# x transposed on the host for the first unit, its rows loaded later, and other banks for the third and fourth units

## What is computed

```python
h = rmsnorm(x, g_mix_pre)
proj = h @ w_in              # q, k, v and the pooled branch u: 2048 columns
q = apply_partial_rope(q, cos, sin); k = apply_partial_rope(k, cos, sin)
mem_n = rmsnorm(mem, g_mem)
kv = mem_n @ w_xkv
```

## Time and profile before

| | us |
|---|---|
| median of 3 runs | 1024.67 |
| lowest, highest | 1023.77, 1025.52 |
| span of the profiled execution, first to last instruction | 1022.5 |
| TensorE busy | 1011.1 |
| VectorE busy | 762.0 |
| ScalarE busy | 538.9 |

### The profile page before, as it was taken

How to read it: one execution, slowest core, us unless ns; L and a number is a source line. 1 busy time by engine, 2 the same in 40 slices (tenths; PEclk the granted TensorE clock), 3 DMA queues, 4 the chain that set the end, 5 groups by cost and what they waited for, 6 DMA issues and landing times.

```text
span 1022.5 us, 17330 instructions
## 1 busy us (share of the span) xinstructions
PE 1011.1 (99%) x6962; PEld 908.8 (89%) x6962; DVE 762.0 (75%) x1040; ACT 538.9 (53%) x757; POOL 31.5 (3%) x49
## 2 busy tenths in 40 slices
PE   8999999999999999999999999999999999999997
PEld 7999899898888889998888888889999988888885
DVE  6987687698886457887788888446788869888632
ACT  6876484565444347765465444326534355554431
POOL 1100100000000001000000000001000100000000
PEclk9999999999999999999999999999999999999999
DMA  9834463266555546533346555555434236555521
GB/s 347 353 128 156 170 225 127 83 232 225 185 202 197 179 159 271 207 125 124 124 147 224 185 185 205 192 183 203 167 142 165 83 126 246 205 191 185 200 83 41
DMA packets 27294, 183.41 MB, mean 179 GB/s; under 512 B 3201, under 2 KB 3473, under 8 KB 6113
## 3 DMA queue, kind: packets, MB, share of 16 engines
q1 hardware_dynamic: 25056, 175.01, 47.6%
q0 software_dynamic: 1744, 7.16, 1.9%
q10 hardware_dynamic: 432, 0.37, 0.1%
HBM read 181.48 MB, written 1.05 MB: 179 GB/s over the span
## 4 chain that ended last, share of the span: by engine, by line
PE 95%; ACT 2%; DVE 1%; issue 1%; ACTq 0%
PE GT L1913 11%; PE D L1913 11%; PE GT L1876 9%; PE GT L1878 9%; PE GT L1877 9%; PE D L1876 8%; PE D L1878 8%; PE D L1877 8%; PE GT L1919 6%; PE D L1919 5%; PE D L2647 1%; PE GT L2083 1%; ACT s_whi L516 1%; PE GT L2141 1%; DVE s_wlo L1031 1%
## 5 line engine op out<-in xcount | busy, mean ns | idle before, releaser
L1031 DVE TENSOR_TENSOR s_wlo<-s_raw,s_whi 128x2048 fp32r<-128x2048 f32 (+1 forms) x164 | 355.4, 2169 | 101.5 <-ACT s_whi L516 100.0
L516 ACT ACTIVATE s_whi<-s_raw 128x2048 fp32r<-128x2048 f32 (+1 forms) x164 | 297.9, 1819 | 141.1 <-PE D L1878 86.1
L1913 PE MATMUL GT<-s_x,s_whi 128*128 128x512 f32 x512 | 124.4, 390 | 0.0
L1913 PE MATMUL D<-s_x,s_whi 128*128 128x512 f32 x480 | 116.4, 390 | 0.0
L1913 PEld LDWEIGHTS GT<-s_x,s_whi 128*128 128x128 f32 x512 | 93.6, 188 | 17.3
L1876 PE MATMUL D<-s_whi,s_hTh 128*128 128x512 f32 x264 | 103.0, 390 | 0.0
L1878 PE MATMUL D<-s_whi,s_hTl 128*128 128x512 f32 x264 | 102.7, 389 | 0.0
L1877 PE MATMUL D<-s_wlo,s_hTh 128*128 128x512 f32 x264 | 102.7, 389 | 0.0
L1913 PEld LDWEIGHTS D<-s_x,s_whi 128*128 128x128 f32 x480 | 87.8, 188 | 16.3
L1876 PE MATMUL GT<-s_x,s_whi 128*128 128x256 f32 x336 | 95.1, 283 | 0.0
L1877 PE MATMUL GT<-s_x,s_whi 128*128 128x256 f32 x336 | 94.1, 280 | 0.0
(11 more groups left out here) (408 smaller groups left out, 1789.6 us busy)
## 6 DMA issues: line engine op xcount, KB each, us to landing
s_raw<-in_stream SPq DMA_DIRECT2D x164, 1024.0 KB, 4.8
s_gb<-in_rows POOLq DMA_DIRECT2D x4, 512.0 KB, 4.0
s_xn<-in_x SPq DMA_DIRECT2D x2, 512.0 KB, 4.3
s_raw<-in_stream SPq DMA_DIRECT2D x4, 256.0 KB, 6.9
s_y<-in_mem POOLq DMA_DIRECT2D x1, 1024.0 KB, 11.7
s_w<-in_cmpw POOLq DMA_DIRECT2D x1, 1024.0 KB, 9.5
s_poolm<-in_poolm POOLq DMA_DIRECT2D x1, 768.0 KB, 14.1
s_retd<-in_retm POOLq DMA_DIRECT2D x1, 768.0 KB, 5.2
```

What stands on the lines that cost most here:

```text
L516: nc.scalar.activation(high(u, n), raw[:, u % RING, 0:n], ACT.Copy)\
L1031: nc.vector.tensor_tensor(low(u, n), raw[:, u % RING, 0:n], high(u, n), ALU.subtract)\
L1913: return nc.tensor.matmul(o[:, f, :], high_block(u, kt, f), x2[:, kt, :], start=start, stop=stop)
```

## The change

The host sends x a second time, transposed (`xT`, features on the partitions). SyncE loads it in four pieces, into the buffer y as `xraw`, then units 1 to 3 with all constants in one DMA, and x by rows last. ScalarE's queue loads the four pieces of unit 0 and the gains. ScalarE and VectorE make `xTh` and `xTl` from SBUF, each piece as it lands; the transposes on TensorE go. The squares of x stand behind the splits of units 1 to 3 on both engines (scratch is now kxT), and so do the means and the powers that need them. Units 2 and 3 are put into banks D0 and D1 and wait for no bank; spreading rstd stands behind unit 3 on TensorE. In three places two DMAs now share one semaphore.

```diff
@@ -161,6 +160,7 @@
         x2 = sb(ctx, "x2", [P, KT, 2 * S], F32R)
+        xraw = y[:].rearrange("p t n -> p (t n)").rearrange("p (k n) -> p k n", k=KT)
         xTh, xTl = x2[:, :, 0:S], x2[:, :, S:2 * S]
...
@@ -347,6 +347,10 @@
 
+        def first_bank(u):
+
+            return (G[0], G[1], DB[0], DB[1])[u]
+
         def pow_at(name):
...
@@ -398,15 +402,14 @@
         def _(sp):
-            for t in range(NT):
-                sp.dma_start(xn[:, t, :], x_in[t * P:(t + 1) * P, :]).then_inc(sem(f"x_in{t}"), 16)
             for i in range(4):
-                sp.dma_start(raw[:, 0, 512 * i:512 * i + 512], stream[0, :, 512 * i:512 * i + 512])\
-                    .then_inc(sem(f"first_in{i}"), 16)
+                sp.dma_start(xraw[:, 2 * i:2 * i + 2, :], xT_in[:, 2 * i:2 * i + 2, :]).then_inc(sem(f"xT_in{i}"), 16)
             for j in range(1, RING):
                 sp.dma_start(raw[:, j, :], stream[j, :, :]).then_inc(landed[j], 16)
                 if j == 1:
-                    sp.dma_start(cst[:, CONST_FIRST:], consts_in[:, CONST_FIRST:]).then_inc(sem("cst_in"), 16)
+                    sp.dma_start(cst[:], consts_in).then_inc(sem("cst_in"), 16)
+            for t in range(NT):
+                sp.dma_start(xn[:, t, :], x_in[t * P:(t + 1) * P, :]).then_inc(sem("x_in"), 16)
             with sp.Fori(1, N_UNITS // RING) as i:
...
@@ -427,7 +430,7 @@
         def _(pool):
-            pool.wait_ge(sem("cst_first_in"), 16)
+            pool.wait_ge(sem("cst_in"), 16)
 
...
@@ -633,17 +636,24 @@
 
-            act.dma_start(cst[:, 0:CONST_FIRST], consts_in[:, 0:CONST_FIRST]).then_inc(sem("cst_first_in"), 16)
-            act.dma_start(gains[:], gains_in[:, 0:LAM]).then_inc(sem("gains_in"), 16)
-            norm_squares(0, xn, lambda c: chunk(y, c), parts=range(2))
+            for i in range(4):
+                act.dma_start(raw[:, 0, 512 * i:512 * i + 512], stream[0, :, 512 * i:512 * i + 512])\
+                    .then_inc(sem(f"first_in{i}"), 16)
+                if i == 0:
+                    act.dma_start(gains[:], gains_in[:, 0:LAM]).then_inc(sem("gains_in"), 16)
+            x_scratch = kxT[:].rearrange("p (c k) n -> p c (k n)", c=4)
             act.wait_ge(sem("gains_in"), 16)
             for i in range(4):
-                norm_hi(0, xTh, (2 * i, 2 * i + 1))
+                act.wait_ge(sem(f"xT_in{i}"), 16)
+                for kt in (2 * i, 2 * i + 1):
+                    nc.scalar.activation(xTh[:, kt, :], xraw[:, kt, :], ACT.Copy, scale=gain("g_mix_pre", kt))\
+                        .then_inc(sem("norm_hi"), 1)
                 act.wait_ge(sem(f"first_in{i}"), 16)
                 nc.scalar.activation(whi[:, 0, 512 * i:512 * i + 512], raw[:, 0, 512 * i:512 * i + 512],
                                      ACT.Copy).then_inc(sem("first_hi") if i < 3 else hi_ready, 1)
             for j in range(1, 4):
                 split(j)
+            norm_squares(0, xn, lambda c: x_scratch[:, c, :], parts=range(2))
             u0 = BASE["in"]
...
@@ -651,7 +661,7 @@
                 for t in range(NT):
-                    ins = nc.scalar.activation(dst[:, t, :], halves(G[bank(u)][:])[:, t, :], ACT.Copy,
+                    ins = nc.scalar.activation(dst[:, t, :], halves(first_bank(u)[:])[:, t, :], ACT.Copy,
                                                scale=rstd[:, POW_COL[f"x0.{t}"]])
...
@@ -1231,16 +1240,14 @@
             nc.vector.memset(gb[:, 0:512], 0.0).then_inc(sem("warm_in"), 1)
-            dve.wait_ge(sem("x_in1"), 16)
-            for c in range(2, 4):
-                nc.vector.tensor_tensor_reduce(chunk(y, c), chunk(xn, c), chunk(xn, c), 1.0 / D, 0.0,
-                                               ALU.mult, ALU.add, ss[:, 16 + c:17 + c])\
-                    .then_inc(sem("norm_sq"), 1)
-            norm_mean(0, "x0", 0)
-            norm_mean(0, "x0", 1)
             dve.wait_ge(sem("gains_in"), 16)
             for i in range(4):
-                norm_lo(0, xTh, xTl, (2 * i, 2 * i + 1))
+                dve.wait_ge(sem(f"xT_in{i}"), 16)
+                dve.wait_ge(sem("norm_hi"), 2 * i + 2)
+                for kt in (2 * i, 2 * i + 1):
+                    nc.vector.scalar_tensor_tensor(xTl[:, kt, :], xraw[:, kt, :], gain("g_mix_pre", kt),
+                                                   xTh[:, kt, :], ALU.mult, ALU.subtract)\
+                        .then_inc(sem("xT_ready"), 1)
                 if i < 3:
...
@@ -1251,6 +1258,14 @@
             split(3)
+            x_scratch = kxT[:].rearrange("p (c k) n -> p c (k n)", c=4)
+            dve.wait_ge(sem("x_in"), 32)
+            for c in range(2, 4):
+                nc.vector.tensor_tensor_reduce(x_scratch[:, c, :], chunk(xn, c), chunk(xn, c), 1.0 / D, 0.0,
+                                               ALU.mult, ALU.add, ss[:, 16 + c:17 + c])\
+                    .then_inc(sem("norm_sq"), 1)
+            norm_mean(0, "x0", 0)
+            norm_mean(0, "x0", 1)
             split(4)
...
@@ -1965,17 +1979,6 @@
 
-            def raw_transposes():
-
-                pe.wait_ge(sem("cst_first_in"), 16)
-                for t in range(NT):
-                    pe.wait_ge(sem(f"x_in{t}"), 16)
-                    for kt in range(KT):
-                        c = S * (kt % 2) + P * t
-                        ins = nc.tensor.transpose(DB[kt // 2][:, c:c + P], xn[:, t, P * kt:P * kt + P], ident)
-                        if t == NT - 1 and kt % 2:
-                            ins.then_inc(sem("norm_tr"), 1)
-
             def first_unit():
...
@@ -2261,28 +2264,27 @@
             nc.tensor.matmul(TB[0][:, 0:256], gb[:, 0:P], gb[:, 0:256], start=True, stop=True)
-            raw_transposes()
             u0 = BASE["in"]
             first_unit()
             second_unit(u0 + 1)
+            for u in (u0 + 2, u0 + 3):
+                wait_unit(u)
+                rows(u, xTh, xTl, o=first_bank(u)).then_inc(unit_done, 1)
+            pe.wait_ge(sem("cst_in"), 16)
             pe.wait_ge(rstd_ready, pow_at("x0.1") + 1)
             for t in range(NT):
                 ins = nc.tensor.matmul(TB[1][:, P * t:P * t + P], rstd[:, POW_COL[f"x0.{t}"]].broadcast_to([P, P]),
                                        ident, start=True, stop=True)
             ins.then_inc(sem("rstd_wide"), 1)
-            unit(u0 + 2, rows)
-            unit(u0 + 3, rows)
             unit(u0 + 4, columns)
             unit(u0 + 5, columns)
-            pe.wait_ge(sem("cst_in"), 16)
             mem_transposes()
             unit(u0 + 6, columns)
             pe.wait_ge(sem("tables_scaled"), 2)
 
             for b in range(2):
                 pe.wait_ge(bank_read[b], bank_reads(u0 + 4)[b])
-            pe.wait_ge(sem("poolm_in"), 16)
-            pe.wait_ge(sem("wpool_in"), 16)
+            pe.wait_ge(sem("pool_in"), 32)
             for g in range(4):
```

More of the change, by code:

```diff
@@ L139, in bank_reads, with build @@
     return n
-def build(nc, stream, x_in, mem_in, pos_in, gains_in, rows_in, consts_in, poolm_in, wpool_in, retm_in,
+def build(nc, stream, x_in, xT_in, mem_in, pos_in, gains_in, rows_in, consts_in, poolm_in, wpool_in, retm_in,
           hgm_in, cmpw_in, cmps_in, out):
@@ L452, in _ @@
             pool.dma_start(y[:], mem_in.rearrange("(t p) d -> p t d", p=P)).then_inc(sem("mem_in"), 16)
-            pool.dma_start(poolm[:], poolm_in).then_inc(sem("poolm_in"), 16)
-            pool.dma_start(wpool, wpool_in).then_inc(sem("wpool_in"), 16)
+            pool.dma_start(poolm[:], poolm_in).then_inc(sem("pool_in"), 16)
+            pool.dma_start(wpool, wpool_in).then_inc(sem("pool_in"), 16)
             pool.dma_start(gb[:], rows_in[0, :].partition_broadcast(P)).then_inc(sem("gb_in"), 16)
@@ L473, in _ @@
             load_row(3, 3)
-            pool.dma_start(rcos[:], retm_in[:, 0:S]).then_inc(sem("rcos_in"), 16)
-            pool.dma_start(rsin[:], retm_in[:, S:2 * S]).then_inc(sem("rsin_in"), 16)
+            pool.dma_start(rcos[:], retm_in[:, 0:S]).then_inc(sem("turns_in"), 16)
+            pool.dma_start(rsin[:], retm_in[:, S:2 * S]).then_inc(sem("turns_in"), 16)
             pool.dma_start(retd[:], retm_in[:, 2 * S:].rearrange("p (h n) -> p h n", h=4))\
@@ L524, in norm_squares @@
                         act.wait_ge(sem("x_part"), 4 * (version - 1) + c + 1)
-                    if n == 0 and c % 2 == 0:
-                        act.wait_ge(sem(f"x_in{c // 2}"), 16)
+                    if n == 0 and c == 0:
+                        act.wait_ge(sem("x_in"), 32)
                     nc.scalar.activation(scratch(c), chunk(src, c), ACT.Square, scale=D ** -0.5,
@@ L536, in tile_hi @@
                         else:
-                            act.wait_ge(sem("norm_tr"), 4 * n + kt // 2 + 2)
+                            act.wait_ge(sem("norm_tr"), 4 * (n - 1) + kt // 2 + 2)
                     col = P * (kt % 4)
@@ L545, in norm_hi @@
                     if kt % 2 == 0:
[L546 removed]
+                        act.wait_ge(sem("norm_tr"), 4 * (n - 1) + kt // 2 + 1)
```

(9 more changed lines are left out.)

1 line of the change is left out of this document (removed).

## The result

| | us |
|---|---|
| before, median of 8 runs | 1024.67 (1023.71 to 1025.52) |
| changed kernel, median of 8 runs | 1027.09 (1025.97 to 1028.08) |
| ratio | 1.0024, 95% interval 1.0015 to 1.0032 |
| profiled execution of the changed kernel: time, span | 1027.69, 1025.5 |

The change makes the kernel 2.4 us slower. The direction was forecast, the size was not: the forecast was 5.2 us. The two profiled executions lie 3.0 us apart; that of the changed kernel took 0.6 us longer than its median.

What follows compares the result with a forecast made beforehand. TensorE, busy 99% of the span, was taken to bound the kernel. 2.8 (chain) + 1.9 (positions) − 0.3 (load) + 0.8 (clock) = 5.2 us slower: 1024.67 + 5.2 = 1029.9 us, range 1026.0 to 1032.5.

Steps and rivals of the forecast that it cites:

- The chain: VectorE's 20 us of work from its split of unit 4 to the first rotary product, starting 3.8 us later.
- rstd's holds: Late rstd delays ScalarE's split of unit 4 by 3.83 us and GpSimd's DMA of the positions, issued at 25.3.
- 2.8: Unit 6 on TensorE waits for VectorE's first rotary product: 3.8 us late with 1.0 to spare.
- − 0.3: Opening load: 0.3 us earlier with two queues at work from the start; bounds 1.3 earlier, 0.3 later.
- The wait for the positions, 1.9: VectorE, ready for the cast at 30.1 us, waits 1.9 for positions landing at 32.0, 6.7 after issue.
- The clock, 0.8 on top of the waits: TensorE's clock falls in its idle stretch from 43.5 to 49.7 us, costing 0.8 us; bounds 0 and 2.8.
- After unit 6 TensorE moves by the same amount.: After unit 6 TensorE is as late as VectorE, and nothing more is lost or regained.
- the second unit starts there, 0.45 earlier than now: TensorE's second unit starts at 14.83 us, when ScalarE has unit 1's high half, 0.45 us earlier than before.
- The rule of the Trainium skill that I weighed: Opening load: transfers from several engines interleave, saving issue time alone; gain nil, total 0.3 us higher.
- the wait for mem: TensorE waits from 43.5 to about 46.5 us for VectorE to scale mem, 3 us.
- Rival 1: Positions land in time and the clock holds: 2.5 us slower, 1027.2 us; chance 0.14.

Runs made afterwards that it cites:

- e2: Changed kernel with ScalarE's split of unit 4 moved ahead of its evacuation of unit 0; 1027.53 us.
- e4: Changed kernel with ScalarE's split of unit 4 ahead of its evacuation of unit 0 and GpSimd's positions and lambdas DMAs ahead of its powers; 1025.83 us.
- e9: Kernel of e6 with VectorE's cast of the positions and angles of the sine ahead of its split of unit 4; 1024.63 us.
- e1: Changed kernel with the four pieces of unit 0 issued by SyncE, each behind its piece of x transposed; 1027.43 us.
- e3: Changed kernel with GpSimd's DMAs of positions and lambdas ahead of its two powers; 1026.69 us.
- e6: Changed kernel with the edits of e1, e2 and e3 together; 1025.44 us.
- e10: Kernel of e9 with ScalarE's table load brought early and six matmuls on zeros in the opening; 1023.29 us.
- e11: Kernel of e9 with the pieces of unit 0 back on ScalarE's queue; 1026.75 us.

## Why the prediction was wrong

**Right.** The chain, nearly to the tenth: rstd at 25.3 (25.2 forecast), the split of unit 4 on ScalarE at 26.12 (25.93) and on VectorE at 28.07 (27.88), the positions issued at 25.23, unit 6 waiting for the first rotary product. e2, e4 and e9 show that both of rstd's holds are real. The first gained copy of x came at 5.57 (5.8), the first matmul at 7.14 (7.2).

**Wrong, the steps that made the number too large.** The sum was 2.8 + 1.9 − 0.3 + 0.8, let through whole to the end. (a) *The wait for the positions, 1.9.* It was 0.56 us. They landed in 5.7 us instead of 6.7, and VectorE was ready 0.3 later than I had it. The fit of the Trainium skill (DMA: Bandwidth & Descriptors, Anatomy of one DMA) gives an estimate of 2.3 us for 128 KB and no wait; the trace does not agree, its 5.7 us being nearer to the row of 6.7, though the wait that came of it was small. (b) *The clock, 0.8 on top of the waits.* In the changed kernel it did not fall at unit 6. In e1 it fell there for 3.4 us, in which 15 matmuls ran against 30 at full speed, and cost about 0.3: VectorE's first rotary product ended at 48.69, and unit 6 began at 49.10, 0.4 behind it, where in the changed kernel it began 0.15 behind (48.55 and 48.70). VectorE set the pace there and went on while TensorE was slow. (c) *"After unit 6 TensorE moves by the same amount."* Unit 6 was 3.66 us late (4.4 forecast), the pool matmuls after it began 54.23 − 50.77 = 3.5 late, and at 130 us 3.07 were left, which is the 3.0 of the two spans. The traces show where the difference went: three stretches of 48 matmuls took TensorE 0.2 us less each than before (unit 6, from its first matmul to the pool matmuls, 5.53 us instead of 5.73). What sets this pace no run shows. The measured 2.4 us is a median, and the profiled run is 0.6 above its own.

**Wrong in the mechanism, the step "the second unit starts there, 0.45 earlier than now".** It started 2.4 later. I had taken the two queues as one, landing bytes in the order in which they are wanted, and bounded the load between 1.3 us earlier and 0.3 later as a whole. As a whole it was that: in e1, on one queue, unit 1 lands at 12.89 as before, and unit 3 lands at 18.41 on two queues and at 18.44 on one. But on two queues the next unit overtook the pieces of the first. The rule of the Trainium skill that I weighed (DMA: Bandwidth & Descriptors, Issuing engines are not separate DMA queues: transfers from several engines interleave on the same engines, and a second issuer saves only the time of issuing) was right, and I drew too little from it: what interleaves also gets in the way. The trace agrees with it: 428 GB/s on two queues from 8 to 11 us against 436 before, shared as 0.37 MB to 1.32 from 8 to 12.

This step did not make the number too large. With TensorE 2.4 us late from the opening, the waits at mem and unit 6 shrank to 1.0 us, and the clock fell at 8.3 us and not there. Where the opening goes nearly as forecast (e1, 15.09), the wait for mem is 2.5 us, near the 3 forecast, and the clock falls at 45.6; yet that kernel takes 1027.4 too. The late opening hid in waits that the chain would have caused anyway.

Rival 1 (a quick load of the positions, a steady clock: 2.5 us slower) gave the number that came, by other means, and that is luck: the positions did come sooner, but TensorE was late from the opening already, and its clock fell there.

## What to carry to other kernels

When a value is made later, look at every list in which something stands behind its first use: before, rstd was first used 11 us after it was ready (at 20.1 and 8.7 us), but ScalarE's next split and GpSimd's next DMA stood behind it, and the two held the same chain, so that freeing one alone gave nothing. Put loads that are wanted in an order on one queue in that order; here a second queue let the large rows of later data pass the small rows of earlier data. And two delays on different engines that meet at one point do not add: price the later one only, expect no gain from repairing the earlier alone (e1), and from repairing the later alone only the distance between them (e4).

## What the runs showed of the hardware

- With most bytes in rows of 8 KB on one queue and rows of 2 KB on another, the first took 1.32 MB and the second 0.37 MB of the same 4 us.
- In the opening, with the first unit stopping and starting, TensorE's clock fell to 1.2 GHz for 3.4 us (e1, e2, e3, e6, e9) or 6.8 (the changed kernel), after TensorE had stood idle for some 1.5 us and again after four matmuls. Six matmuls on zeros in the gaps kept it at 2.4 in the profiled run of e10. In e4 and e11 the matmuls ran at the pace of 1.2 GHz until about 14.3 us while the granted clock read 1.00.
- The stretch at 1.2 GHz near 422 us costs 1.4 to 1.6 us. By the profiled runs and the mean clock of each run, it is there in some runs of a kernel and not in others, and in no run of e10; a microsecond between two medians can be that.
